# Final norm of one late tile of token rows moved from VectorE to ScalarE and GpSimd in a fused pooling, MoE and RMSNorm kernel

## The reference

```python
h = rms_norm(x, norm_mix[0])
x = x + pool_mixer(h, pool_w[0], pool_scale[0])
x = x + hier_moe(rms_norm(x, norm_ffn[0]), router_group_w[0], router_group_b[0],
                 router_expert_w[0], router_expert_b[0], expert_w_gu[0], expert_w_down[0])
return rms_norm(x, norm_final)

def rms_norm(x, w):
    y = x * lax.rsqrt(jnp.mean(x * x, axis=-1, keepdims=True) + NORM_EPS)
    return y * w
```

## Time and profile before

| | |
|---|---|
| Median of 3 runs | 686.91 us (686.42 to 687.38) |
| The profiled execution | 686.19 us, of which the span of the profile is 684.4 us |
| Mean granted TensorE clock | 0.988 |
| TensorE busy | 660.6 us, 97% of the span |
| VectorE busy | 606.6 us, 89% |
| ScalarE busy | 528.0 us, 77% |
| GpSimd busy | 244.0 us, 36% |
| DMA | 242.62 MB, mean 354 GB/s |
| Chain that ended last, by engine | PE 87%, DVE 5%, DMA 3%, ACT 3%, issue 2% |

### The profile page before, as it was taken

One profiled execution on the slowest core, in us unless ns is written; L12 is line 12 of the kernel. 1 busy time (PEld: TensorE's weight loads), 2 busy tenths in 40 slices (PEclk: granted clock), 3 DMA queues, 4 the chain that ended last, 5 costly groups with the idle time before them and its releaser, 6 DMA issues.

```text
span 684.4 us, 10289 instructions
## 1 busy us (share of the span) xinstructions
PE 660.6 (97%) x3638; PEld 558.1 (82%) x3638; DVE 606.6 (89%) x470; ACT 528.0 (77%) x446; POOL 244.0 (36%) x194
## 2 busy tenths in 40 slices
PE   6899989999999999999999999999999999999992
PEld 4899978788888888888888888888888888888881
DVE  6896779888888888899899889988889989898987
ACT  6995527777777788777777888778878888888894
POOL 3000013044444444444444333444433535452401
PEclk9999989999999999999999999999999999999997
DMA  8997859999999999999999999994999999999865
GB/s 301 417 420 250 259 189 420 384 360 380 392 381 373 375 380 388 385 367 385 369 382 387 380 387 388 396 386 147 337 368 379 384 382 386 378 389 382 300 261 202
DMA packets 45155, 242.62 MB, mean 354 GB/s; under 512 B 9719, under 2 KB 10879, under 8 KB 20546
## 3 DMA queue, kind: packets, MB, share of 16 engines
q1 hardware_dynamic: 34322, 220.39, 82.6%
q0 software_dynamic: 10800, 21.80, 11.5%
HBM read 230.34 MB, written 29.36 MB: 379 GB/s over the span
## 4 chain that ended last, share of the span: by engine, by line
PE 87%; DVE 5%; DMA 3%; ACT 3%; issue 2%; POOL 0%; SPq 0%; ACTq 0%; DVEq 0%; POOLq 0%
PE psum L1520 73%; PE psum L1540 4%; PE psum L1448 3%; PE psum L1551 2%; PE psum L1434 2%; PE psum L1466 2%; DMA xg<-normed,src_all 1%; DMA pw_in<-in_pool_w 1%; PE psum L1474 1%; PE psum L1457 1%; DVE raw L1342 1%; ACT end_junk L731 1%; DVE pw L1045 0%; DMA out<-raw 0%; PE psum L1510 0%
## 5 line engine op out<-in xcount | busy, mean ns | idle before, releaser
L1086 DVE TENSOR_TENSOR w_lo<-raw,w_hi 128x2048 fp32r<-128x2048 f32 x152 | 345.4, 2290 | 32.3 <-ACT w_hi L799 32.0
L799 ACT ACTIVATE w_hi<-raw 128x2048 fp32r<-128x2048 f32 x152 | 288.0, 1915 | 26.6 <-PE psum L1520 26.6
L1520 PE MATMUL psum<-w_lo,x_hi 128*128 128x512 f32 x616 | 182.7, 392 | 0.0
L651 POOL DMA_INDIRECT total<-ysb,dst_now x29 | 60.5, 2086 | 221.4 <-ACT ysb L879 221.4
L1520 PEld LDWEIGHTS psum<-w_lo,x_hi 128*128 128x128 f32 x616 | 115.1, 188 | 24.8 <-issue 0.5
L1520 PE MATMUL psum<-w_hi,x_hi 128*128 128x512 f32 x408 | 129.5, 399 | 0.0
L1520 PE MATMUL psum<-w_hi,x_lo 128*128 128x512 f32 x408 | 126.0, 390 | 0.0
L1086 DVE TENSOR_TENSOR w_lo<-raw,w_lo 128x2048 fp32r<-128x2048 f32 x40 | 89.9, 2287 | 5.4 <-ACT w_lo L799 5.3
L1520 PE MATMUL psum<-w_lo,h_hi 128*128 128x512 f32 x312 | 92.8, 393 | 0.0
L1520 PEld LDWEIGHTS psum<-w_hi,x_lo 128*128 128x128 f32 x408 | 76.6, 188 | 16.7
L1520 PEld LDWEIGHTS psum<-w_hi,x_hi 128*128 128x128 f32 x408 | 72.9, 188 | 16.7 <-DVE w_lo L1086 3.5
(11 more groups left out here) (156 smaller groups left out, 778.8 us busy)
## 6 DMA issues: line engine op xcount, KB each, us to landing
raw<-in_expert_w_gu SPq DMA_DIRECT2D x128, 1024.0 KB, 8.1
raw<-in_expert_w_down SPq DMA_DIRECT2D x64, 1024.0 KB, 7.3
res<-in_x SPq DMA_DIRECT2D x8, 512.0 KB, 9.4
normed<-nx POOLq DMA_DIRECT2D x8, 512.0 KB, 8.1
total<-res SPq DMA_DIRECT2D x8, 512.0 KB, 9.0
raw<-total SPq DMA_DIRECT2D x8, 512.0 KB, 8.3
out<-raw SPq DMA_DIRECT2D x8, 512.0 KB, 3.8
pw_in<-in_pool_w SPq DMA_DIRECT2D x1, 1024.0 KB, 7.7
```

The costliest lines, as they stand in the source:

```text
L651: pool.indirect_dma_start(out=total[:, :], out_offset=bass.IndirectOffsetOnAxis(ap=dst_now[:].bitcast(u32), axis=0), in_=ysb[:], in_offset ...
L799: nc.scalar.activation(hi_at(s0, j), raw[q][:], ACT.Copy).then_inc(hi_done, 1)
L1086: V.tensor_tensor(w_lo[q][:], raw[q][:], hi_at(s0, j).bitcast(f32), ALU.subtract)\
L1520: last = mm(dst[:, n * N:(n + 1) * N], a[:, ch, :], b[:, c * D + n * N:c * D + (n + 1) * N], start=(ch == 0 and a is hi and b is b_hi), st ...
```

## The change

The tile of step 29 (`late_tile(0)`) is no longer normed by VectorE's `late_norm(0)`. ScalarE makes its squares and root earlier, between `final_square(4)` and `final_square(5)`. VectorE still takes the reciprocal, now between `final_norm(4)` and `final_norm(5)`. ScalarE multiplies the tile by the reciprocal in place, between `final_square(6)` and `final_square(7)`. GpSimd multiplies it by `nfin` in place, ahead of its wait for `out_stored`. GpSimd's first store then waits for its own product in place of `late_made`, and the other two stores for `late_made` 1 and 2. Line numbers of the changed kernel are larger than those of before by 3 to 18.

```diff
@@ names of semaphores
+        late_rooted = sem("late_rooted")
+        late_scaled = sem("late_scaled")
+        late_weighed = sem("late_weighed")
@@ GpSimd
             for k in range(LATE):
                 pool.indirect_dma_start(out=late_tile(k), out_offset=None, in_=total[:, :], in_offset=late_rows(k),
                                         bounds_check=TOKENS - 1, oob_is_err=False).then_inc(late_in[k], 16)
+            pool.wait_ge(nfin_in, 16)
+            pool.wait_ge(late_scaled, 1)
+            nc.gpsimd.tensor_tensor(late_tile(0), late_tile(0), nfin[:], ALU.mult).then_inc(late_weighed, 1)
             pool.wait_ge(out_stored, 16 * TILES)
             for k in range(LATE):
-                pool.wait_ge(late_made, k + 1)
+                if k == 0:
+                    pool.wait_ge(late_weighed, 1)
+                else:
+                    pool.wait_ge(late_made, k)
@@ ScalarE
             for i in range(4, TILES):
                 final_square(i, 0)
-            for k in range(LATE):
+                if i == 4:
+                    late_squares(0)
+                if i == 6:
+                    act.wait_ge(late_rooted, 1)
+                    nc.scalar.activation(late_tile(0), late_tile(0), ACT.Identity, scale=rs2[:, 0:1])\
+                        .then_inc(late_scaled, 1)
+            for k in range(1, LATE):
                 late_squares(k)
@@ VectorE
             for i in range(3, TILES):
+                if i == 5:
+                    dve.wait_ge(late_square, 1)
+                    V.reciprocal(rs2[:, 0:1], rs2[:, 0:1]).then_inc(late_rooted, 1)
                 if i == 6:
                     late_add(1, Y, MAIN - GU_PAIRS // 2)
                 final_norm(i, 0)
             late_add(2, GU, MAIN)
-            for k in range(LATE):
+            for k in range(1, LATE):
                 late_norm(k)
```

## The result

The changed kernel takes 689.08 us (median of 9 runs, 688.19 to 690.18), the kernel before in the same session 686.91 us. The ratio, estimated over all runs and not the quotient of the two medians, is 1.0036, with a 95% interval of 1.0026 to 1.0046: slower, and clear of noise. The medians differ by 2.2 us; the interval goes from 1.8 to 3.2 us. The forecast was 688.9 us, slower.

A forecast was written before the change was run, and what follows sets the result against it. The end was taken as bound by the norming of the last total tile. Removed late norm 0, scaling 0, root wait and GpSimd product together +2.0 us (0.31 the wait): 686.91 + 2.0 = 688.9 us, range 687.1 to 690.0.

The forecast's parts named there:

- What bounds the end: End of the kernel: set by when the last of eight total tiles is normed; a fixed 11.18 us follows.
- hidden tail: VectorE's work after 674.5 us, hidden by DMA and GpSimd's stores with 1.18 us slack; removing a late norm gains 0.
- ScalarE's order: ScalarE near the end: squares of tiles 5, 6 and 7 come 1.37 us later, with the scaling before tile 7's.
- The root's delay: VectorE's final_norm(5) waits for its tile's later root, and everything behind it shifts by +0.31 us.
- The scaling: ScalarE's scaling from 670.59 us takes 1.1 us and costs 0; 0.3 us more would just begin to show.
- The product on GpSimd: GpSimd's product from 671.85 us holds VectorE's final_norm(6) product until 673.85: 2.0 us late, the root's 0.31 included.
- T: Length of GpSimd's two-input product of the late tile, taken as 2.0 us, between bounds of 1.1 and 3.3.
- The rule it hung on: VectorE instructions with two SBUF inputs and GpSimd instructions reading SBUF exclude each other throughout; final_norm is held, the deciding term.
- rival 2: GpSimd's product takes 3.3 us and holds VectorE until 675.15: +3.3 us, 690.2 us; chance 0.10.
- Rival 1: VectorE's final_norm isn't held, only the root's wait remains: 687.2 us; chance 0.23, including a short product (1.1 us, 688.0).
- What is late next: Behind tile 7 everything shifts alike by 2.0 us; last late norm done by 680.8, third store 683.1; no new wait.
- rival 3: End hangs on VectorE's last late norm, at GpSimd's third store: 1.09 to 1.40 us gained, 685.5 to 685.8; chance 0.05.

The follow-up runs named there:

- e6: Changed kernel with final_norm and late_norm both reading the final weight from PSUM instead of SBUF; 686.86 us against 686.55 before, ratio 1.0006.
- e9: Kernel before with late_add(1) behind final_norm(7) and all VectorE norms reading the weight from PSUM, nothing shared; 685.94 us against 686.34, ratio 0.9994.
- e8: e6 with late_add(1) behind final_norm(7), the late square behind tile 5's and the scaling behind tile 7's square; 685.83 us, ratio 0.9986.
- e2: Changed kernel with only final_norm reading the final weight from PSUM, copied there by ScalarE; 686.83 us against 686.33 before, ratio 1.0012.
- e10: Changed kernel with GpSimd multiplying the late tile by the constant 1, one input instead of two; 687.69 us against 686.34 before, ratio 1.0023.
- e7: Kernel before with late_add(1) moved behind final_norm(7), nothing else; 686.23 us against 686.55 before, ratio 0.9995.
- e1: Changed kernel with GpSimd's product held back until all eight tiles are normed; 687.72 us against 686.33 before, ratio 1.0024.
- e5: Changed kernel with a second, unused two-input product on GpSimd right behind the first; 690.21 us against 686.55 before, ratio 1.0047.

## Why the prediction was right

*What bounds the end.* Right. The first late store is still released by the landing of the last `out<-raw`, and the norm that was removed was in the hidden tail: in e6, where it is gone and nothing is held, the stretch is still 0.33 us longer than before, and e9 against e8 agrees with 0 for it too.

*ScalarE's order.* Right. The root's delay cost 0.29 us of the 0.31 forecast; e6, where little else is left, has 0.33. The scaling took 1.14 us where 1.1 was taken and delayed nothing. The room it had was smaller than the 0.3 us named: by the prediction's own times tile 7's root is done at 673.17 and needed at 673.33.

*The product on GpSimd.* The mechanism was right, the term too small. T was taken as 2.0 us from the slope of a one-input row, and measured 2.35; the estimate of 2.25 from the Trainium skill (GPSIMD Engine Reference, section 3.1) was nearer. It began 0.14 us after the scaling, as forecast, and before VectorE's product of tile 6. That product was 1.90 us too long, where 1.7 followed from T = 2.0. The nearness is in part luck: T was 0.35 too small, but VectorE's product ended 1.08 us after GpSimd's, not the full 1.28 that the prediction added, and these 0.20 took back over half of the error.

*The rule it hung on.* That the hold applies to a SCALAR_TENSOR_TENSOR was given 0.72 (the forecast and rival 2) on the ground of a copy against a TENSOR_TENSOR. e2 beside the changed kernel shows it, and that it depends on where the second input lies. Rival 1 falls with that, and rival 2 (T = 3.3) with the measured T. That the one who comes second waits for the other's whole instruction held for GpSimd's two-input product, not for the one-input instruction of e10.

*What is late next.* Here the prediction failed in a small thing: "no new wait". The first late store's issue moved from just ahead of a VectorE product to inside one, and cost 0.20 us (0.15 by e2 against e6). The evidence was there: the earlier trace rows show a gather's issue take 1.99 us beside such an instruction. I used them for the product and not for the stores.

*The sum.* 0.29 + 1.90 + 0.20 = 2.39 against 2.37 in the profiles. The forecast 2.0 lacked 0.20 for the product and 0.20 for the store and had 0.02 too much for the root. The median's 2.17 lies nearer to it, but the interval, 1.8 to 3.2 us, cannot tell 2.0 from 2.4. The chances of rival 3 rested on the third late store; e7 shows that when the tiles come earlier it is the first late store that a late norm releases, by 0.16 us.

## What to carry to other kernels

Before moving a product from VectorE to an idle GpSimd, list what VectorE runs in that time, and where its two inputs lie: if both are in SBUF, the engines take turns, as here, and the offload costs VectorE most of its own length (1.90 us of 2.35). One operand in unused PSUM lifted it here for one copy on ScalarE, whose price didn't show. And ask first whether the work removed was late: here it sat behind a DMA landing, and even the share without holds gained nothing.

## What the runs showed of the hardware

- GpSimd's two-input f32 product of 128x1024 takes 2.35 us when it starts first, VectorE's product of the same shape 1.28. Beside each other, with both inputs of VectorE's in SBUF, VectorE's ends 1.08 us after GpSimd's (changed kernel, e1, e5).
- A VectorE product of two SBUF tiles draws out the issue of GpSimd's indirect DMAs too: 1.02 us outside, 1.21, 1.36 and 2.01 us when begun 0.97, 0.82 and 0.16 us after the product's start (changed kernel, e7, e1), and 1.02 inside one with a PSUM input (e6). The earlier in the product, the longer; the issue ended 0.9 us after the product each time.
- The last of several 512 KB stores landed after 3.03 us when tiles 5 and 6 were normed 2.6 us apart and tile 7 1.4 us later, and within 2.98 to 3.04 in all runs with `late_add(1)` in its place. With the three tiles 1.4 to 1.7 us apart it took 3.58, 3.71 and 4.03 us (e7, e8, e9). Why, and why these three differ, stays open.
